# Modulation, norm and input projections of a diffusion layer: one block in place of three

## What is computed

```python
sh1, sc1, g1, sh2, sc2, g2 = split(silu(cond) @ ada_w + ada_b, 6)   # cond: c for latent, c_ctx for context tokens
u = rms_norm(x, norm_pre_mix) * (1 + sc1) + sh1
p = u @ w_in            # columns: q, k, v of 512, then 5 x 256 and 256
...                     # attention, recurrence, pooling, projection
x = x + g1 * rms_norm(mix @ w_out, norm_post_mix)
u = rms_norm(x, norm_pre_ffn) * (1 + sc2) + sh2
...                     # expert feed-forward
x = x + g2 * rms_norm(ff, norm_post_ffn)
```

## Time and profile before

| | us |
|---|---|
| median of 3 runs | 3457.57 |
| lowest, highest | 3457.2, 3462.61 |
| the profiled execution | 3458.87 |
| its span, first to last instruction | 3457.2 |

### The profile page before, as it was taken

The page is one execution under the profiler, slowest core; times in us unless marked ns, Lnnn a source line. Parts: engine busy times, 40 slices in busy tenths (PEclk is TensorE's granted clock), DMA queues, the critical chain, the costliest instruction groups (busy, mean ns, idle before and its releaser), DMA issues. The chain is left out here.

```text
span 3457.2 us, 52889 instructions
## 1 busy us (share of the span) xinstructions
PE 2947.5 (85%) x20103; PEld 2551.3 (74%) x20103; DVE 1732.9 (50%) x3539; ACT 1207.8 (35%) x2110; POOL 772.3 (22%) x1256
## 2 busy tenths in 40 slices
PE   8679999995988788787899339999999999999980
PEld 1258788884766566576687329999999999999980
DVE  2442203323544366672444575666666666666634
ACT  0441214321444433341333014444444444444422
POOL 3013400004555233461011000112211111111111
PEclk9679999996999888788899559999999999999995
DMA  7334542246777320211433235566666656556528
GB/s 269 139 123 140 180 146 83 96 155 152 178 173 170 111 71 28 88 55 45 147 111 116 104 127 168 173 186 184 185 197 184 193 171 188 179 171 193 174 71 326
DMA packets 312148, 513.98 MB, mean 149 GB/s; under 512 B 56206, under 2 KB 197558, under 8 KB 310296
## 3 DMA queue, kind: packets, MB, share of 16 engines
q1 hardware_dynamic: 283050, 410.22, 37.5%
q0 software_dynamic: 24336, 85.48, 8.7%
q10 hardware_dynamic: 4592, 16.06, 1.3%
HBM read 404.96 MB, written 122.52 MB: 153 GB/s over the span
## 5 line engine op out<-in xcount | busy, mean ns | idle before, releaser
L2499 DVE TENSOR_TENSOR ex_wlow<-ex_w,ex_whigh 128x2048 fp32r<-128x2048 f32 x192 | 440.1, 2293 | 158.8 <-ACT ex_whigh L2439 158.6
L2439 ACT ACTIVATE ex_whigh<-ex_w 128x2048 fp32r<-128x2048 f32 x192 | 366.9, 1912 | 252.9 <-DMA ex_w<-in_w_up 141.5
L2319 POOL DMA_INDIRECT ff_rows<-ex_YR,ex_sel_out x32 | 82.3, 2572 | 1081.3 <-DVE ex_YC L2491 1076.4
L2327 PE MATMUL ex_Y<-ex_hs_high,ex_whigh 128*128 128x272 f32 x1024 | 303.0, 296 | 17.1 <-DVE ex_hs_low L2515 17.1
L2327 PE MATMUL ex_G<-ex_xs_high,ex_whigh 128*128 128x272 f32 x1024 | 301.3, 294 | 2.3 <-DVE ex_xs_low L2483 2.3
L2329 PE MATMUL ex_G<-ex_xs_high,ex_wlow 128*128 128x272 f32 x1024 | 297.4, 290 | 0.0
L2329 PE MATMUL ex_Y<-ex_hs_high,ex_wlow 128*128 128x272 f32 x1024 | 297.2, 290 | 0.0
L2327 PE MATMUL ex_U<-ex_xs_high,ex_whigh 128*128 128x272 f32 x1024 | 296.9, 290 | 0.0
L2329 PE MATMUL ex_U<-ex_xs_high,ex_wlow 128*128 128x272 f32 x1024 | 296.6, 290 | 0.0
L2328 PE MATMUL ex_G<-ex_xs_low,ex_whigh 128*128 128x272 f32 x1024 | 295.6, 289 | 0.0
L2328 PE MATMUL ex_Y<-ex_hs_low,ex_whigh 128*128 128x272 f32 x1024 | 295.5, 289 | 0.0
(11 more groups left out here) (366 smaller groups left out, 7185.8 us busy)
## 6 DMA issues: line engine op xcount, KB each, us to landing
ex_w<-in_w_gate SPq DMA_DIRECT2D x64, 1024.0 KB
ex_w<-in_w_up SPq DMA_DIRECT2D x64, 1024.0 KB
ex_w<-in_w_down SPq DMA_DIRECT2D x64, 1024.0 KB
wada<-in_ada_w SPq DMA_DIRECT2D x12, 2048.0 KB, 8.2
hg_rows<-hg_pool_rows SPq DMA_DIRECT2D x68, 256.0 KB, 3.0
at_k_high<-key_parts SPq DMA_DIRECT2D x64, 256.0 KB, 4.1
hg_pool_rows<-hp_res POOLq DMA_DIRECT2D x34, 384.0 KB, 2.8
hp_w<-in_w_in SPq DMA_DIRECT2D x48, 256.0 KB
```

The lines of the kernel that those rows point to most:

```text
L2319: pool.indirect_dma_start(ff_d, bass.IndirectOffsetOnAxis(ap=sel_out[0:n, i:i + 1], axis=0), src, None, compute_op=ALU.add).then_inc(s_sc, 16)
L2327: nc.tensor.matmul(out, wh, xh, start=start, stop=False)
L2439: nc.scalar.activation(h, v, ACT.Copy).then_inc(s_high, 1)
L2499: nc.vector.tensor_tensor(l, v, h, ALU.subtract).then_inc(s_low, 1)
```

## The change

The three functions become one, `trunk_in`, with one block. What moves:

- Small vectors (conditioning, norms, `ada_b`) are loaded by ScalarE's queue into 96 rows and transposed at once; Silu is applied to the first 16 rows.
- Of `ada_w` only the four chunks of the first shift and scale are loaded as chunks, between the first eight weight pieces on SyncE's queue. On TensorE they are now the stationary operand (128 x 128 at a time), the two conditioning columns move, and the results are columns at once.
- All 17 x tiles have room of their own; the tiles from 9 on lie where the masks are made, so they are loaded when the masks are stored.
- The norm of the first four tiles stands ahead of the products, that of each following pair behind the first and second query product of a token group (`tiles_after`, `to_features`). The queries go by token group first.
- The other eight chunks are loaded in 64 pieces of 128 x 512 through the ring of the projection weights, two in each of four of five steps, from the first key step on. VectorE multiplies each by the conditioning value of its partition and adds it to one of two rows (`add_columns`, two instructions for each piece). Behind each chunk TensorE sums over the partitions by a product with a column of ones (`later_columns`, eight of them).
- The cached keys are transposed two ahead of each half of the keys. The gates are made as columns, transposed, and stored.

The core of it:

```diff
-        modulation(nc, g, a, gates, masks_d)
-        with Mem(nc) as mu:
-            g.uH, g.uL = mu.sb("u_high", [P, KD, N_TOK], F32R), mu.sb("u_low", [P, KD, N_TOK], F32R)
-            norm_transpose(nc, g, a)
-            projections(nc, g, a, out, q_d, k_d, v_d, hgp, pads, bias_q, bias_k, v_w)
+        trunk_in(nc, g, a, out, gates, masks_d, q_d, k_d, v_d, hgp, pads, bias_q, bias_k, v_w)
...
-        first_steps = [(b, f, c) for b in (QB, KB) for f in range(C // P) for c in range((N_TOK + 511) // 512)]
-        first_steps += [(KB, f, CACHED) for f in range(C // P)]
+        first_steps = [(QB, f, c) for c in range(NC) for f in range(NF)]
+        for half_f in range(2):
+            pair = range(2 * half_f, 2 * half_f + 2)
+            first_steps += [(KB, f, CACHED) for f in pair] + [(KB, f, c) for f in pair for c in range(NC)]
...
+        ADA_FROM, ADA_CHUNKS = LAST_OF[QB] + 1, 8
+        NEXT_AT = NF * (NC - 1) - 2
+        def ada_at(s):
+            q, i = divmod(s - ADA_FROM, 5)
+            return [8 * q + 2 * i, 8 * q + 2 * i + 1] if 0 <= q < ADA_CHUNKS and i < 4 and s < M else []
+        ring = [("w", x, None) for x in range(KD)]
+        for s in range(len(blocks)):
+            ring += [("w", x, s) for x in pieces_at(s)] + [("ada", j, s) for j in ada_at(s)]
...
             def _(sp):
+                def load_piece(y):
+                    if y >= LOADS:
+                        kind, x, _ = ring[y - LOADS]
+                        if kind == "w":
+                            sp.wait_ge(s_wl, x + 1)
+                        else:
+                            sp.wait_ge(s_acc, 2 * x + 2)
...
+                    sp.dma_start(w[:, y % LOADS, :], src).then_inc(s_w[y % LOADS], 16)
+                for t in range(4):
+                    load_x(t)
+                for y in range(3):
+                    load_piece(y)
+                load_ada(0)
+                for y in range(3, 6):
+                    load_piece(y)
+                load_ada(1)
+                for y in range(6, KD):
+                    load_piece(y)
+                load_ada(2)
+                load_ada(3)
+                for t in range(4, MASK_TILES.start):
+                    load_x(t)
+                sp.wait_ge(s_bands, 2)
+                sp.wait_ge(s_cur, 1)
+                sp.dma_start(masks_d, masks).then_inc(s_mout, 16)
+                sp.wait_ge(s_mout, 16)
+                for t in range(MASK_TILES.start, TILES):
+                    load_x(t)
...
             def _(pe):
+                def later_columns(q):
+                    pe.wait_ge(s_acc, 16 * (q + 1))
+                    for i in range(4):
+                        for r in range(2):
+                            o = 2 * (4 * q + i) + r
+                            last = nc.tensor.matmul(mc2[:, o:o + 1], acc[:, r, i * P:(i + 1) * P], g.ones[:, 0:1], start=True, stop=True,
+                                                    skip_group_check=True)
+                    last.then_inc(s_red, 1)
+                pe.wait_ge(s_silu, 1)
+                nc.tensor.transpose(cps[:, 0:96], crow, g.ident[0:96, 0:96]).then_inc(s_ct, 1)
+                for t in range(2):
+                    to_features(t)
+                pe.wait_ge(s_col, 1)
+                for c in range(4):
+                    pe.wait_ge(s_ada[c], 16)
+                    for i in range(4):
+                        o = 2 * (4 * c + i)
+                        for k in range(KD):
+                            last = nc.tensor.matmul(mc1[:, o:o + 2], wada[:, c, k, i * P:(i + 1) * P], colT[:, k:2 * KD:KD],
+                                                    start=(k == 0), stop=(k == KD - 1), skip_group_check=True)
+                last.then_inc(s_mc, 1)
+                for t in range(2, 4):
+                    to_features(t)
...
+                        if s > ADA_FROM and (s - ADA_FROM) % 5 == 4 and (s - ADA_FROM) // 5 < ADA_CHUNKS:
+                            later_columns((s - ADA_FROM) // 5)
...
             def _(dve):
+                def add_columns(j):
+                    q, k = j // 8, j % 8
+                    src, loaded, count = slot_of("ada", j)
+                    dve.wait_ge(loaded, count)
...
+                    for r in range(2):
...
+                        nc.vector.scalar_tensor_tensor(out=acc[:, r, :], in0=src, scalar=colT[:, r * KD + k:r * KD + k + 1],
+                                                       in1=acc[:, r, :], op0=ALU.mult, op1=ALU.add).then_inc(s_acc, 1)
...
+                for t in range(4):
+                    rows_normed(t)
+                for x in range(3):
+                    low_part(x)
+                dve.wait_ge(s_bands, 1)
+                for gi in range(len(WINDOWS)):
+                    fill_pool_cur(nc, g, pom, band, ti, tf, cnt, gi, link)
+                nc.vector.memset(done[:, :], 0.0).then_inc(s_cur, 1)
+                for x in range(3, KD):
+                    low_part(x)
+                dve.wait_ge(s_col, 1)
+                dve.wait_ge(s_mc, 1)
...
                 for n in range(M):
                     for x in pieces_at(n):
                         low_part(x)
+                    for j in ada_at(n):
+                        add_columns(j)
...
+                    if blocks[n] == QB:
+                        tiles_after(n)
```

More of the change, by code:

```diff
@@ L465, in projections, with trunk_in @@
[L465 removed]
+def trunk_in(nc, g, a, out, gates, masks_d, q_d, k_d, v_d, hgp, pads, bias_q, bias_k, v_w):
     C = 512
@@ new lines, in trunk_in @@
+        s_small, s_silu, s_ct, s_col, s_mc, s_mod = (m.sem("mod_" + x) for x in ("small", "silu", "ct", "col", "mc", "mod"))
+        s_ada = [m.sem(f"mod_ada{i}") for i in range(4)]
+        s_acc, s_red, s_fin, s_gcol, s_gt, s_grow, s_gout = (m.sem("mod_" + x) for x in ("acc", "red", "fin", "gcol", "gt", "grow", "gout"))
+        s_pc, s_bands, s_dc, s_cur, s_mout = (m.sem("mask_" + x) for x in ("pool", "bands", "dve", "cur", "out"))
+        s_x = [m.sem(f"n_x{i}") for i in range(TILES)]
+        s_sq, s_root, s_rs, s_xn, s_t = (m.sem("n_" + x) for x in ("sqd", "root", "rs", "xn", "t"))
@@ L612, in _ @@
+                later_cached = False
+                for y in range(KD, len(ring)):
+                    kind, x, s = ring[y]
+                    if kind == "w" and x == KD:
+                        for f in range(2):
+                            load_cached(f)
                         sp.wait_ge(s_pz, 1)
@@ new lines, in evacuate @@
+                def evacuate(t):
+                    if t == 0:
+                        act.wait_ge(s_mod, 1)
+                    act.wait_ge(s_t, 2 * t + 2)
+                    if t >= UR:
+                        act.wait_ge(s_ul, t - UR + 1)
+                    for k in range(4, 8):
+                        nc.scalar.activation(u[:, t % UR, k, :], tp[(2 * t + 1) % 4][:, (k - 4) * P:(k - 3) * P],
+                                             ACT.Identity, bias=g.shift[:, 0, cond(t), k:k + 1],
+                                             scale=g.scale[:, 0, cond(t), k:k + 1]).then_inc(s_ua, 1)
@@ new lines, in _ @@
+                dve.wait_ge(s_fin, 2)
+                nc.vector.scalar_tensor_tensor(out=g.scale[:, 0], in0=mtmp[:, :, :], scalar=1.0, in1=norm_cols(slice(16, 24)),
+                                               op0=ALU.add, op1=ALU.mult).then_inc(s_mod, 1)
+                dve.wait_ge(s_mod, 1)
+                for pair in (0, 1), (2, 3):
+                    for t in pair:
+                        evacuate(t)
+                    for t in pair:
+                        token_low(t)
+                for t in range(4, 8):
+                    rows_normed(t)
```

511 lines of the change are left out of this document (235 added, 276 removed).

## The result

| | before | changed |
|---|---|---|
| median of the runs compared (4 each) | 3458.39 | 3434.78 |
| lowest, highest | 3457.2, 3462.61 | 3426.18, 3435.78 |
| the profiled execution | 3458.87 | 3426.18 |
| its span | 3457.2 | 3424.2 |

The changed kernel takes 0.9919 of the time before, 95% interval 0.9906 to 0.9931: faster by 23.6 us of median, where 64 were forecast. 3434.8 lies 7 above the range of 3362 to 3428. The sign was right, the size was not.

The account below looks back on a forecast made before the run. The prediction took TensorE's projection products, held back to 209.5 us, as the bound: -117.5 - 2.9 + 13.4 + 37.5 + 5.4 = -64, from 3457.6 to 3394 us. Own range 3376 to 3412; 3362 to 3428 with most rivals.

Parts of the forecast that it names:

- The start: First projection product would start at 92 us instead of 209.5, with ada products at the lower clock: -117.5 us.
- the first rival: Ada products ahead of the first product run at the higher clock: first product at 82, 3384 us; chance 0.17.
- Queries: Query products: -2.9 us from ready weights, +13.4 for transposes of tiles 4 to 16, engine work hidden.
- The ramp: Start of the queries: some eight matmuls at half the clock, 1.6 us.
- Keys: Key stretch where later weights are summed: 25 us waits, 9 column sums, 10 lower clock, less 7: +37.5 us.
- three waits at some 3.3: Keys: clock falls after three waits, slowing column sums and a few matmuls behind them: +10 us.
- Values and the rest: Values and behind: VectorE's sums run ahead, only three column sums are added: +5.4 us.
- from the values on the old pitch of 5.44: From the value products on, each long product would take 5.44 us as before.
- The sums keep ahead: Keys: loads come back sooner than chained, the 25 and most of the 10 go: 3362 us; chance 0.11.
- Stores land later: Keys: late stores delay VectorE's subtractions, 16 steps by 1 to 2 us each: 3414, to 3428; chance 0.13.
- Not hidden at all: Later weights' sums: 64 pieces, 83 us, all ahead of column sums: about 3450, no change; chance 0.04.
- slower: Clock stays at 0.50 in queries and keys; queries and half the keys so would give 3544 us; chance 0.04.

Follow-up runs that it names:

- E1: The changed kernel run again unaltered, with a second profile, as yardstick for the other runs: 3430.78 us, 0.9913 of the kernel before.
- E6: Changed kernel plus 48 wide products (128x512) in TensorE's idle time ahead of modulation chunk 2: 3428.55 us, 0.9907 of the kernel before.
- E2: Changed kernel with each of the eight column sums one step later in TensorE's list: 3394.13 us, 0.9809 of the kernel before.
- E3: Changed kernel with fourteen of each chunk's sixteen adds narrowed to 16 of 512 columns: 3413.37 us, 0.9864 of the kernel before.
- E12: Changed kernel with the eight pairs of bias table transfers sixteen steps later, behind the values: 3421.42 us, 0.9885 of the kernel before.
- E7: Changed kernel with 32 bytes left free ahead of the second group of weight places: 3426.97 us, 0.9902 of the kernel before.
- E11: Changed kernel with 32 bytes left free ahead of the first group of weight places instead: 3436.55 us, 0.9934 of the kernel before.
- E8: Changed kernel with the column sum a step later and each chunk's pieces taken in three steps: 3387.31 us, 0.9788 of the kernel before.
- E9: Changed kernel with E7's and E8's edits and the low parts ahead of the pooling masks: 3367.65 us, 0.9729 of the kernel before.
- E4: Changed kernel without the later modulation weights: no loads, adds or column sums: 3360.82 us, 0.9715 of the kernel before.
- E10: E9 plus four wide products ahead of each eight products of the first modulation columns: 3396.22 us, 0.9818 of the kernel before.

## Why the prediction was wrong, step by step

**The start, -117.5 forecast, -110.4 measured: right in mechanism, short by 7.** The chain was as written: the Silu at 9.8 (8.5 taken), low parts till 20.4 (19), the four masks 27.4 us (26.3), the chunks issued at 49.4 (47.4), chunk 2 landed at 59.7 (55). So 4.7 us up to the landing, 2.0 of them at the issue already, and 2.5 from a chunk of 13.7 instead of 12.5 us. The choice of the lower clock was right (0.50 in E1's row); E6 shows that even the higher one did not last, and with that the first rival (3384) falls. The Trainium skill ("TensorE: Matmul & The Clock Gate", section "LDWEIGHTS (loading the stationary operand)") gives the time of a load by its columns, which makes 107 ns for 128 (an estimate worked out from its formula). The 0.11 of E6's first 37, at a granted clock of 0.99, agrees; the 0.21 at 0.50 is twice that.

**Queries, +10.5 forecast, +9.3 measured: right.** The four groups hid ScalarE's and VectorE's work; TensorE never waited there. The ramp, put at eight matmuls at half the clock, was that: 8 passes start from 99.1 to 102.3 us, at a granted clock of 0.50, and from there on it is 1.00.

**Keys, +37.5 forecast, +48.7 measured: the waits right, the price of a wait too low.** The chain gave waits of 9.6, 0.3, 8.3, 3.7 and 3.5; they were 12.1, 0.8, 9.0, 3.6 and 3.3, together 28.7 instead of 25, and E2 and E3 show that the reason given (the adds stand behind the splits of the step before) was the right one. Failed: the terms beside them. Column sums at 1.8 and "three waits at some 3.3" for the clock make 19; measured are 15.4 for the sums and 10.7 for the products behind, 26.1, since four waits and not three brought the clock down, and each cost 1.7 us in the sum and some 2.6 in the product behind it: some 17 us where the term had 10. By the Trainium skill's rule on waits between bursts ("TensorE: Matmul & The Clock Gate", section "HAM oscillation — how this bites in real kernels") I had counted 13 in place of 10: it was nearer, and still too low. The rest is under 1 us, with the pitch of 5.52 (1.3 us over 16 products) in it.

**Values and the rest, +5.4 forecast, +22.0 measured: this step failed.** "VectorE has no subtractions there, its sums run ahead." True of VectorE, not of the ring that feeds it. The sum counted no transfer beside the pieces; eight pairs of bias tables, 872 KB each pair, go out on ScalarE's queue in these very steps, in the kernel before too, where TensorE did 21 products in 114.2 us without a wait. One wait of 8.0 came of it, with 4 us of clock behind it; E12 moves the tables and the wait is gone. The other failed term is "from the values on the old pitch of 5.44": 5.55 in 17 value products and 34 of the last two blocks, 5 to 6 us, from a split of one weight buffer into two, the second of which begins 32 bytes off (E7, E11). I had read that line of the diff as an edit at no cost.

**The sum.** 7.1 - 1.2 + 11.2 + 16.6 = 33.7 us too few: -64 becomes -30.3, and -30.4 is what the block gained. The stages behind moved along as said, but for the recurrent passes, whose few us in either direction the range had not held. As far as E1 shows, they also make the gap between the block's 30.4 and the 23.6 of the medians: there the block gained 32.1, and the stages behind it took 7.6 more than before.

**The rivals.** "The sums keep ahead" was not the case, but it was one edit away: E8, and E9 with 3367.7, reach nearly its 3362. "Stores land later" gave a time near the measured one for a wrong reason: the stores of the keys landed in 3.2 us (median), in E4, without the loads, in 3.0, so 0.2 and not 1 to 2 us later; and in E2, with all the loads, TensorE waits for none of them. "Not hidden at all" is out by the waits, 36.7 us in all where it had 83, "slower" by the clock, 0.99 in the queries and 0.83 in the keys.

## What to carry to other kernels

When work on a second engine is hidden behind a first one, ask how many steps the first may run ahead of it, not only whether there is time: a sum taken one step later was worth 37 us here, more than taking most of the adds' work away (17, E3). List all queues that issue in a stretch before calling it free, and price a short wait of TensorE with the lower clock behind it: about 4 us more here. A buffer that is split or moved should be looked at for where it begins.

## What the runs showed of the hardware

- A group of operand buffers of the matrix products cost some 3% by where it began: 0.233 to 0.236 us a pass of 128x512 in place of 0.227, as the stationary operand (keys, E11's queries) and as the moving one (values). 32 bytes left free ahead of it take the cost away (E7) or bring it to the other group (E11). That the slow place is 32 bytes above a multiple of 64 is counted from the kernel's list of buffers; the traces show no addresses, and no other offset was tried.
- The granted clock is shown as 1.00 until the first record of it in a trace: 92.0 us in the first profile of the changed kernel, 18.5 in E1. Under that 1.00 the products took the time of the lower level; E1 and E6 show 0.50 for the same products at the same pace.
- While products of two moving columns ran without a gap the clock fell from its upper level (E6, at 64 us), and with bursts of four wide products between them it did not come up again (E10, 0.50 from 25 to 90 us).
- A wait of TensorE of 1.2 us, ahead of E2's sixth sum, was followed by 0.50 from 375.2 to 382.0 us; a wait of 0.84 us in the changed kernel was not.
- A pair of transfers of 504 and 368 KB on ScalarE's queue held up 256 KB pieces on SyncE's: 7.2 us from issue to use against some 3.5; without the pair the same pieces landed in 2.8 to 3.2 us, and ScalarE's longest wait for a piece in these steps fell from 4.5 to 1.5 us (E12).
